# A two-block transformer kernel: the first stage starts with the memory's values, on a new plan of raw slots

## The reference, cut to what matters

```python
# keys and values of the memory (second block), needed only at the end
mem_n = rms_norm(mem, norm_mem_g)
mkv = jnp.einsum('bmd,de->bme', mem_n, w_mem_kv[layer])
mk, mv = jnp.split(mkv, 2, axis=-1)
...
# modulation of layer 0 (first block)
mod_l = c_act @ ada_w[i] + ada_b[i]
mod_c = cc_act @ ada_w[i] + ada_b[i]
h_l = _rms_norm(x, norm_gain[i]) * (1 + sc_l[:, None]) + sh_l[:, None]
h_c = _rms_norm(ctx, norm_gain[i]) * (1 + sc_c) + sh_c
...
# values of retention head 0, the first product that needs h
p = h @ w_in
```

## Time and profile before

| | us |
|---|---|
| median of three runs | 3170.6 |
| lowest, highest | 3167.61, 3170.93 |
| profiled execution, its own time | 3171.53 |
| its span, first to last instruction | 3170.1 |
| mean granted TensorE clock | 0.995 |

### The profile page before, as it was taken

One profiled execution on the slowest core, in us unless ns is written; L12 is line 12 of the kernel. 1 busy time (PEld: TensorE's weight loads), 2 busy tenths in 40 slices (PEclk: granted clock), 3 DMA queues, 4 the chain that ended last, 5 costly groups with the idle time before them and its releaser, 6 DMA issues.

```text
span 3170.1 us, 47439 instructions
## 1 busy us (share of the span) xinstructions
PE 3104.5 (98%) x19672; PEld 2742.8 (87%) x19672; DVE 1994.0 (63%) x3330; ACT 1282.7 (40%) x1854; POOL 0.2 (0%) x4
## 2 busy tenths in 40 slices
PE   8999999999999999999999999999999999999998
PEld 6677788888888888888878889988999999999998
DVE  5543466757666676575757577768776665555555
ACT  4443323232322323232236465556554444444443
POOL 0000000000000000000000000000000000000000
PEclk9999999999999999999999999999999999999999
DMA  9854533434434344343423234436555555555564
GB/s 370 305 204 179 196 123 120 159 120 134 139 115 152 112 153 146 113 145 120 148 87 113 93 114 153 143 130 216 178 171 182 169 165 174 181 195 195 189 197 149
DMA packets 154645, 511.02 MB, mean 161 GB/s; under 512 B 15552, under 2 KB 36160, under 8 KB 153664
## 3 DMA queue, kind: packets, MB, share of 16 engines
q1 hardware_dynamic: 149904, 495.13, 46.8%
q10 hardware_dynamic: 4528, 12.86, 1.1%
HBM read 503.72 MB, written 4.21 MB: 160 GB/s over the span
## 4 chain that ended last, share of the span: by engine, by line
PE 90%; DVE 5%; ACT 3%; DMA 1%; issue 1%; ACTq 0%; DVEq 0%
PE bank L641 29%; PE bank L643 28%; PE bank L642 28%; DVE w_lo L1772 1%; PE bank L703 1%; DMA raw<-stream 1%; PE bank L921 1%; ACT w_hi L1168 1%; ACT a_s L1478 1%; PE bank L867 0%; DVE a_s L2208 0%; DVE a_numbers L2218 0%; ACT a_s L1420 0%; ACT a_pt L1491 0%; PE bank L881 0%
## 5 line engine op out<-in xcount | busy, mean ns | idle before, releaser
L641 PE MATMUL bank<-h_hi,w_hi 128*128 128x256 f32 (+1 forms) x4032 | 1255.7, 311 | 9.3 <-DVE w_lo L1772 4.6
L643 PE MATMUL bank<-h_hi,w_lo 128*128 128x256 f32 (+1 forms) x4032 | 1240.6, 308 | 0.0
L642 PE MATMUL bank<-h_lo,w_hi 128*128 128x256 f32 (+1 forms) x4032 | 1240.3, 308 | 0.0
L1772 DVE TENSOR_TENSOR w_lo<-raw,w_hi 128x1024 fp32r<-128x1024 f32 x729 | 882.2, 1221 | 417.1 <-ACT w_hi L1168 414.5
L1168 ACT ACTIVATE w_hi<-raw 128x1024 fp32r<-128x1024 f32 x729 | 761.8, 1056 | 890.1 <-PE bank L643 781.1
L641 PEld LDWEIGHTS bank<-h_hi,w_hi 128*128 128x128 f32 x4032 | 760.5, 189 | 66.5 <-issue 21.4
L642 PEld LDWEIGHTS bank<-h_lo,w_hi 128*128 128x128 f32 x4032 | 760.6, 189 | 46.2 <-issue 3.4
L643 PEld LDWEIGHTS bank<-h_hi,w_lo 128*128 128x128 f32 x4032 | 760.4, 189 | 43.0
L641 PE MATMUL bank<-w_hi,h_hi 128*128 128x512 f32 x704 | 284.0, 403 | 12.8 <-DVE w_lo L1772 5.9
L643 PE MATMUL bank<-w_hi,h_lo 128*128 128x512 f32 x704 | 276.1, 392 | 0.0
L642 PE MATMUL bank<-w_lo,h_hi 128*128 128x512 f32 x704 | 275.7, 392 | 0.0
(11 more groups left out here) (274 smaller groups left out, 3058.8 us busy)
## 6 DMA issues: line engine op xcount, KB each, us to landing
raw<-stream SPq DMA_DIRECT2D x904, 512.0 KB, 4.1
raw_h<-stream SPq DMA_DIRECT2D x32, 512.0 KB, 10.4
res<-tokens_in ACTq DMA_DIRECT2D x4, 1024.0 KB, 8.9
vg<-mem_in ACTq DMA_DIRECT2D x4, 512.0 KB, 8.7
c_rows<-cond_rows SPq DMA_DIRECT2D x4, 512.0 KB, 4.3
h_hi<-mem_kv ACTq DMA_DIRECT2D x2, 1024.0 KB, 10.0
out<-res SPq DMA_DIRECT2D x4, 512.0 KB, 3.0
mem_kv<-qk ACTq DMA_DIRECT2D x1, 1024.0 KB, 8.5
```

The costliest lines, as they stand in the source:

```text
L641: pe.matmul(out, sh, mh, start=start, stop=False, **checks)
L642: pe.matmul(out, sh, ml, start=False, stop=False, **checks)
L643: return pe.matmul(out, sl, mh, start=False, stop=stop, **checks)
L1772: dve.tensor_tensor(in_quarters(m.low(raw)[:, :]), m.raw[SLOT[raw]], in_quarters(m.w_hi[slot][:, :]).bitcast(F32), ALU.subtract).then_inc( ...
```

## The change

The first stage is put in another order. The memory's values come first, then its keys, then head 0's values as before. `mv` chunk 0 needs only two k tiles of the memory, so the memory is loaded in eight transfers of two k tiles each, on SP's queue, each put between the chunks of the stream (`MEM_IN`); ACT and DVE split the k tiles two at a time between the weight chunks, and the squares and sums follow behind. The root of the memory's mean square moves to the second half of `mv`. The decay logarithms and the constants of DVE move behind the first steps. The four token transfers move to the second half of `mv`, the token squares to the keys, the two copies of memory keys and values out to device memory to step 5 of `v`, the tables' loads to step 6.

There are twenty raw slots: the sixteen of before, two in the first half of the memory's own buffer (free once its first eight k tiles are split), two where the tables will be loaded. A slot is the one that was used longest ago among those allowed at that chunk (`slots_for`): twenty up to the last key chunk, twelve after it, six from eight chunks before `qk`.

The 64 modulation chunks are shared out anew: none before the first product (before: 3), 16 beside `mv` (before: 27), 22 beside `mk` (before: 16), 26 beside `v` (before: 18).

```diff
 BESIDE = {"start": modulation_beside(
-    [(("begin",), 3)]
-    + [(("mk", i, j), 1) for i in range(8) for j in range(2)]
-    + [(("mv", 0, c), 1 + c % 2) for c in range(8)]
-    + [(("mv", 1, c), n) for c, n in enumerate((1, 1, 1, 2, 1, 2, 1, 6))]
-    + [(("v", i), n) for i, n in enumerate((5, 5, 4, 4, 0, 0, 0, 0))],
+    [(("mv", n, c), 1) for n in range(2) for c in range(8)]
+    + [(("mk", i, j), 1 + (j if i % 4 else 0)) for i in range(8) for j in range(2)]
+    + [(("v", i), n) for i, n in enumerate((6, 5, 5, 5, 5, 0, 0, 0))],
...
+RAW_SLOTS = 20
+MEM_SLOTS, TABLE_SLOTS = (16, 17), (18, 19)
+TABLE_SLOTS_END = WHERE["v", 0][4]
+def slots_for(c):
+    if c >= EARLY:
+        return range(SLOTS)
+    out = list(range(SLOTS, WIDE))
+    if c < EARLY - WIDE:
+        out += range(SLOTS)
+    if c <= WHERE["mk", 7][1]:
+        out += range(WIDE, 2 * WIDE)
+    if c >= 2 * WIDE + len(TABLE_SLOTS):
+        out += MEM_SLOTS
+    if c < TABLE_SLOTS_END:
+        out += TABLE_SLOTS
+    return out
...
+        if c in MEM_IN:
+            i = MEM_IN[c]
+            sp.dma_start(m.mem_raw[:, 2 * i:2 * i + 2, :], d["mem_in"][:, 2 * i:2 * i + 2, :]).then_inc(s.load[f"mem_in{i}"], 16)
+        if c == MEM_FREED:
+            sp.wait_ge(*s["h_lo"].at("mem", 7))
+            sp.wait_ge(*s["squared"].at("mem", 7))
...
         for c in range(8):
+            if n == 0:
+                pe.wait_ge(*s["h_lo"].at("mem", 2 * c + 1))
             values_chunk(("mv", n), outs, c)
+            if (n, c) == (0, 0):
+                pe.wait_ge(*s["cond_done"].at())
+            if (n, c) == (1, 0):
+                memory_means()
...
+    memory_high(0)
+    weights_to(WHERE["mv", 0][0], 1)
+    for n in range(2):
+        for c in range(8):
+            if n == 0 and c < 7:
+                memory_high(c + 1)
+            weights_to(WHERE["mv", n][c], SLOTS if n else 2)
+            if n == 0:
+                memory_squares(c)
...
+            beside("start", "mv", n, c)
+            if n == 1 and c % 2 == 0:
+                tokens_in(c // 2)
+    for n in range(8):
+        for half in range(2):
+            weights_to(WHERE["mk", n][half])
...
+            if n == 7:
+                for k in (2 * half, 2 * half + 1):
+                    h_mods(0, k, m.h_t0)
             beside("start", "mk", n, half)
...
+    act.wait_ge(s.mm, DONE[WHERE["mk", 7][1]])
+    for k in range(4):
+        h_high(0, k, m.h_t0)
```

More of the change, by code:

```diff
@@ L398, in __init__ @@
         self.hi, self.lo, self.mm = sem("hi"), sem("lo"), sem("mm")
-        self.raw = [sem(f"raw{i}") for i in range(2 * WIDE)]
+        self.raw = [sem(f"raw{i}") for i in range(RAW_SLOTS)]
         self.load = {name: sem(f"load_{name}") for name in LOADS}
@@ L756, in between @@
         def between(half):
-            if (n, half) == (0, 1):
-                memory_means()
+            if (n, half) == (4, 1):
+                mean("x0", BOTH)
             beside("start", "mk", n, half)
         return between
[L761 to L764, removed]
     for n in range(2):
@@ L1927, in vector_program, with constants @@
-    weights_to(WHERE["mk", 0][0], 2)
-    beside("start", "begin")
+    def constants():
+        dve.memset(m.ones_mean[:, :], 1.0 / D_MODEL)
+        dve.memset(m.ones_dv[:, :], 1.0 / RET_DV)
+        dve.tensor_scalar(m.half_gain[:, :], m.param("ret_gain"), 0.5, None, ALU.mult).then_inc(*s["tables_set"].up())
+        for layer in range(DEPTH):
+            i = dve.tensor_scalar(m.bias1[:, layer, :], m.param(f"ada_b{layer}", KT, KT), 1.0, None, ALU.add)
+        i.then_inc(*step.up("bias1"))
+        dve.wait_ge(*step.at("bias1"))
@@ new lines, in memory_low @@
+    def memory_low(i):
+        for k in (2 * i, 2 * i + 1):
+            dve.wait_ge(s.load[f"mem_in{i}"], 16)
+            dve.wait_ge(*s["h_hi"].at("mem", k))
+            dve.scalar_tensor_tensor(out=m.h2_lo[:, k, SIDE], in0=m.mem_raw[:, k, :], scalar=m.param("mem_gain", k, 1),
+                                     in1=m.h2_hi[:, k, SIDE].bitcast(F32), op0=ALU.mult, op1=ALU.subtract
+                                     ).then_inc(*s["h_lo"].up("mem", k))
+    memory_low(0)
+    weights_to(WHERE["mv", 0][0], 1)
@@ new lines, in vector_program @@
+    for n in range(2):
+        for c in range(8):
+            if n == 0 and c < 7:
+                memory_low(c + 1)
+            weights_to(WHERE["mv", n][c], SLOTS if n else 2)
+            if n == 0:
+                for k in (2 * c, 2 * c + 1):
+                    add_square("mem", k, SIDE)
+            if (n, c) == (0, 2):
+                constants()
+            if (n, c) == (1, 0):
+                decay_logs()
+            if (n, c) == (1, 1):
+                reciprocal(("mem_means",), m.mem_rstd[:, :], ("mem_means",))
+                reciprocal(("mean", "mem"), m.o_rstd[:, LAT], ("mem",))
+            beside("start", "mv", n, c)
@@ L1940, in vector_program @@
-            beside("start", "mk", n, half)
-    for n in range(2):
-        for c in range(8):
-            weights_to(WHERE["mv", n][c])
-            if n == 0:
-                for k in (2 * c, 2 * c + 1):
-                    add_square("x0", k, BOTH)
-            if (n, c) == (1, 3):
+                dve.tensor_tensor(m.mem_k[:, n, :], psum("mk", n)[:, LAT], m.o_rstd[:, LAT], ALU.mult
+                                  ).then_inc(*banks.up("mk", n))
+            if (n, half) == (6, 0):
                 dve.wait_ge(*s["rstd"].at("x0"))
@@ L1950, in vector_program @@
                 h_raws(0, 1, m.h_t0)
-            beside("start", "mv", n, c)
-            if (n, c) == (1, 1):
+            beside("start", "mk", n, half)
+            if (n, half) == (4, 1):
                 reciprocal(("mean", "x0"), m.rstd[:, :], ("x0",))
```

198 lines of the change are left out of this document (85 added, 113 removed).

## The result

| | before | after |
|---|---|---|
| median (lowest, highest; 14 runs each) | 3171.9 (3167.6, 3175.7) | 3178.1 (3175.7, 3181.3) |
| span of the profiled execution | 3170.1 | 3176.7 |
| head 0's queries start in it | 213.23 | 218.16 |

The ratio is 1.0022 (95% interval 1.0015 to 1.0030). Predicted were 3172.8 us, range 3161 to 3179, with "the same" as the likeliest sign. The time lies in the range, 5.3 us above the forecast; it is above 3176.9, so the sign is "slower", to which I had given 0.21.

The account below looks back on a forecast made before the run. PE was taken as the bound, busy 3104.5 of 3170.1 us. Terms -7.2 + 5.1 + 2.1 + 0.3 + 1.2 + 0.8 = +2.3 took the profiled 3171.5 to 3173.8, less 0.9 over the median: 3172.8 us, range 3161 to 3179.

Parts of the forecast that it names:

- the same: Whole kernel: time between 3164.3 and 3176.9 us, not told from no change; chance 0.57.
- Start: Kernel start: without eight split k tiles ahead, PE's first product comes at 8.4 us; -7.2 us.
- First group: First modulation group in `mv`: ACT's copy waits behind chunk 14's high part, PE idle 3.6 and 1.5 us; +5.1 us.
- Tokens: Second half of `mv`: four token transfers, 10.9 us of DMA, stay hidden; nothing lost.
- the fourth rival: Token transfers starve `mv` by sharing DMA evenly: up to 3 us idle, 3175.8 us; chance 0.05.
- Keys to values: From keys to head 0's values: fewer slots, PE idle 6.2 to 6.3 us against 4.19 before; +2.1 us.
- Head 0's values: In `v`: third chunk waits for `w_lo`, +0.3 us; longer wait at the seventh chunk, +1.2 us.
- Clock: First stage: half of 1.6 us lost to 1.2 GHz behind the new order's third idle place; +0.8 us.
- Sum: Whole first stage: all terms together +2.3 us; queries were to start at 212 to 217 us.
- The first (gain kept): Rival: the start's gain stays, as ACT is never held by chunks not landed; 3159 to 3164.8 us; chance 0.26.
- The second (values run dry): Rival: twelve slots and DMA cannot feed head 0's values, ending 6 to 8 us later, 3179 to 3181; chance 0.16.

Follow-up runs that it names:

- last copy: Changed kernel, with `ada_part` of the sixteenth modulation group asking for one chunk ahead instead of four; 3172.2 us.
- last key tile: Changed kernel, ninth group asking for one chunk ahead, and weights of the last key tile's second half split after head 0's first `h_hi` and `h_lo`; 3168.0 us.
- sixteen slots: Changed kernel without the added raw slots: sixteen up to the last key chunk, eight after it, four from chunk 96 on; 3187.4 us.
- old shares: Changed kernel with modulation chunks shifted back: 30 beside `mk`, 18 beside `v`, 16 beside `mv` as in the changed kernel; 3168.7 us.
- The undone copy: Changed kernel, with `ada_part` of the first modulation group asking for one chunk ahead instead of four, so ACT copies that group early; 3173.8 us.
- all three: Changed kernel with one chunk ahead for the first, ninth and sixteenth groups, and the last key tile's weights split later; 3160.4 us.

## Why the prediction was right or wrong, step by step

- **Start, -7.2.** First product at 9.09, not 8.4, and outside the 7.5 to 8.5 named as its sign: -6.5. Right in mechanism, 0.7 off.
- **First group, +5.1.** 4.12 + 0.58 = 4.7, ended by the copy as forecast. Place off: 32.9, not 27.8 to 31.4. Chunk 14 landed at about 31.4, not 29.0 to 29.8: two chunks and a memory pair (1.31 MB) came every 3.7 us (24.07, 27.76, 31.52), 0.355 MB/us, where I had counted on 0.383. PE was late by as much, so the wait came out right by two errors, and by some luck: in four kernels that have the same code up to there (last copy, last key tile, sixteen slots, old shares) PE came to it earlier and the two waits were 5.8 to 6.5 us. The undone copy showed the cause, and that the wait partly moves to the next groups.
- **Tokens, 0.** No idle place between 45 and 75 us. Right; the fourth rival is out.
- **Keys to values, +2.1.** 4.41 + 1.07 - 4.19 = +1.3. Right in mechanism.
- **Head 0's values, +0.3 and +1.2.** 1.09 - 1.36 = -0.3, and 1.50 + 5.20 - 4.94 = +1.8. Right as far as idle time goes.
- **Clock, +0.8. This is the step that failed.** It was +3.3 by the slow rows, +4.0 by PE's own time. I had priced the low clock as 1.6 us per wait, given half of it to the one new wait, and nothing to the other places. Measured, before and after: at the start 4.1 and 2.6, which is -1.5, since the three modulation chunks that ran at half clock there (1.08 us each) are gone; near 33 nothing and 2.5; between keys and values 1.7 and 3.6; ahead of the seventh chunk 1.5 and 1.9. The price of 1.6 holds for a wait with no second one behind it (1.5, 1.7 and 1.9). What the rows of before hid: behind the waits of 4.12 and 4.41 the clock is low at once, the thin work up to the second, short wait (turn 0.98 for 0.58, two modulation chunks in 1.93 for 1.07) then also runs at half speed, and the low clock lasts on into the next matmuls: ten at 1.2 GHz behind 146.44, seven or eight before, behind 148.34 and 180.40.
- **Sum.** Idle time +0.95 against +1.5, PE's own time +4.0 against +0.8: +4.9 against +2.3, so the queries started at 218.16, just outside the 212 to 217 named. With 1.7 us of scatter in the one profile, 6.6; the medians differ by 6.2.
- **Rivals.** The first (gain kept) needed early copies; it came true only in edited kernels. The second (values run dry) did not happen in the changed kernel; with four slots in the last eight chunks it does, 13.74 us at once. What it blamed, 26 chunks beside `v`, cost 9.4 us against the 3.6 that my steps had for that region, since I priced neither the clock nor the work that the keys lacked.

## What to carry to other kernels

An engine's look-ahead loop must not stand ahead of a small copy that another engine is waiting for: ask for one chunk, copy, then look ahead. In this kernel a wait of PE of 4 to 5 us cost 1.5 to 1.9 us more in matmuls at half clock behind it, and 2.5 to 3.6 where a second, short wait followed. Price both. Judge a new order of chunks only after such waits are gone: this one costs 6 us with them and gains 10 without.

## What the runs showed of the hardware that was not expected

Short waits lowered the clock in some places and not in others. Two waits of 1.45 and 1.44 us with 1.2 us of thin work between them were followed by about seven matmuls at 1.2 GHz (36.41 to 39.7). Many single waits of 1.34 to 1.65 us, all ahead of a `v` chunk, were not. But single waits of 1.92 us (first copy early, at 60.78), of 1.67 (all three, at 76.42) and of 1.61 (old shares) were. The last of these, in which four modulation chunks take 3.25 us, where 1.93 is their time at full clock:

```profile
170.48 0.88 PE L746 MATMUL bank<-par,part 128*128 128x2 f32 x4 [1.61 <-ACT part L1230]
171.28 3.25 PE L730 MATMUL bank<-raw,cond 128*32 128x256 f32 x32
```

And the same wait in the same code, behind the queries, was followed by full clock in the profile of before (2.02 us) and by 1.2 GHz in that of the changed kernel (2.03 us). So for waits of 1.6 to 2 us the length alone does not decide; what does is open. Sixteen microseconds of matmuls with 32 columns of weights kept the clock at 2.4 GHz.

Four matmuls of the modulation, each into its own quarter of the output's 128 partitions, take 0.43 us together; one matmul of the same size after the other into the same quarter takes 0.44 us each. The Trainium skill, page "TensorE: Matmul & The Clock Gate", section "Why this matters for your kernels", says that matmuls with an output of fewer than 128 partitions gain when each writes to its own group of 32 of them; it gives 2.38 times for three. The two rows agree, with a gain close to four for four.
